# Opening, four feed-forward stages and two mixing stages in one block, the next stage's first products between the two turnings

## The reference, cut to what matters

```python
for l in range(2):                                   # first block
    x = layer_norm(ALPHA * x + 0.5 * ((silu(x @ ffn1_w1[l]) * (x @ ffn1_w3[l])) @ ffn1_w2[l]), ln1_g[l], ln1_b[l])
    h = x @ w_in[l]                                  # 1024 x 3360, split into the inputs of three mixers
    mix = concatenate([spatial_gating(..), gated_deltanet(..), gla(..)], -1) @ w_out[l]
    x = layer_norm(ALPHA * x + mix, ln2_g[l], ln2_b[l])
    x = layer_norm(ALPHA * x + 0.5 * ((silu(x @ ffn2_w1[l]) * (x @ ffn2_w3[l])) @ ffn2_w2[l]), ln3_g[l], ln3_b[l])
# second block: one layer
mod = silu(c) @ w_ada + b_ada                        # 1024 -> 6144: shifts, scales and gates
x = x + gate1 * attention(rms_norm(x) * (1 + scale1) + shift1)
y = x + gate2 * moe(rms_norm(x) * (1 + scale2) + shift2)   # 32 experts, 4 for each token, 1024 -> 2048 -> 1024
```

## Time and profile before

| | before |
|---|---|
| median of 3 runs | 2237.27 us (2235.18 to 2241.88) |
| the profiled execution's own time | 2240.23 us |
| its span, first to last instruction | 2238.5 us |
| mean granted TensorE clock | 0.996 |
| PE busy in the span | 2167.5 us (97%) |

### The profile page before, as it was taken

One profiled execution on the slowest core, in us unless ns is written; L12 is line 12 of the kernel. 1 busy time (PEld: TensorE's weight loads), 2 busy tenths in 40 slices (PEclk: granted clock), 3 DMA queues, 4 the chain that ended last, 5 costly groups with the idle time before them and its releaser, 6 DMA issues. The chain is left out here.

```text
span 2238.5 us, 30473 instructions
## 1 busy us (share of the span) xinstructions
PE 2167.5 (97%) x12481; PEld 1340.7 (60%) x12482; DVE 1025.8 (46%) x1421; ACT 726.6 (32%) x1121; POOL 92.1 (4%) x139
## 2 busy tenths in 40 slices
PE   8999999999999999999999999999999999999997
PEld 7887877888888887788877743333333333333332
DVE  5665686865666468766559642111111111111111
ACT  5443333643444243354335631111111111111111
POOL 5000020000000001100001000000000000000000
PEclk9999999999999999999999999999999999999999
DMA  9773422687386443158736669999999999999998
GB/s 308 237 237 98 151 78 72 227 284 243 104 298 223 151 145 114 40 185 273 240 129 186 244 277 423 428 429 428 428 429 428 429 428 428 429 428 428 429 429 336
DMA packets 192726, 632.40 MB, mean 283 GB/s; under 512 B 31280, under 2 KB 127552, under 8 KB 166256
## 3 DMA queue, kind: packets, MB, share of 16 engines
q1 hardware_dynamic: 192624, 630.93, 73.1%
HBM read 629.82 MB, written 1.07 MB: 282 GB/s over the span
## 5 line engine op out<-in xcount | busy, mean ns | idle before, releaser
L426 PE MATMUL banks<-ffn_room 128*128 128x512 f32 x1824 | 430.4, 391 | 0.0
L426 PEld LDWEIGHTS banks<-ffn_room 128*128 128x128 f32 x1824 | 339.5, 188 | 69.0
L546 DVE TENSOR_TENSOR ffn_room<-memory,ffn_room 128x2048 fp32r<-128x2048 f32 x132 | 298.7, 2291 | 92.9 <-ACT ffn_room L505 92.9
L3196 DVE TENSOR_SCALAR attend_words<-banks 128x512 f32<-128x512 f32 x32 | 22.1, 692 | 560.5 <-PE banks L2932 560.5
L505 ACT CAST ffn_room<-memory 128x2048 fp32r<-128x2048 f32 x132 | 247.1, 1905 | 68.5 <-PE banks L444 63.4
L444 PE MATMUL banks<-ffn_room 128*128 128x512 f32 x1056 | 248.1, 390 | 0.3
L2932 PE MATMUL banks<-memory 128*64 128x512 f32 x1088 | 242.7, 594 | 0.0
L444 PEld LDWEIGHTS banks<-ffn_room 128*128 128x128 f32 x1056 | 197.6, 188 | 42.7 <-DVE ffn_room L588 2.1
L2932 PEld LDWEIGHTS banks<-memory 128*64 128x64 f32 x1088 | 75.2, 135 | 150.6 <-issue 148.3
L2932 PE MATMUL banks<-attend_later,memory 128*64 128x512 f32 x672 | 152.1, 594 | 0.1
L511 ACT ACTIVATE memory<-banks 128x256 f32<-128x256 f32 x88 | 34.0, 386 | 324.6 <-PE banks L426 305.6
(11 more groups left out here) (478 smaller groups left out, 2780.1 us busy)
## 6 DMA issues: line engine op xcount, KB each, us to landing
memory<-in_ffn_w SPq DMA_DIRECT2D x132, 1024.0 KB, 7.5
memory<-in_w_gate_up SPq DMA_DIRECT2D x62, 2048.0 KB, 22.4
attend_later<-in_w_gate_up SPq DMA_DIRECT2D x39, 2048.0 KB, 23.9
memory<-in_w_down SPq DMA_DIRECT2D x25, 2048.0 KB, 24.2
attend_later<-in_w_down SPq DMA_DIRECT2D x19, 2048.0 KB, 23.0
attend_words<-in_w_gate_up SPq DMA_DIRECT2D x17, 2048.0 KB, 22.4
memory<-in_w_in SPq DMA_DIRECT2D x32, 1024.0 KB, 6.6
memory<-in_w_ada SPq DMA_DIRECT2D x32, 768.0 KB, 5.6
```

Source lines behind the costliest of these rows:

```text
L426: m = nc.tensor.matmul(psum[:, GU + tt, :], x_parts[:, xp, k, tt * P:tt * P + P], rows, start=(n == 0), stop=(n == 3 * KD - 1))
L546: tt_op(b, chip.ring[:, chip.slot(base + i), :], a.bitcast(F32), ALU.subtract).then_inc(chip.used, 1)
L3196: ts(room.gate, psum[:, GATE_BANK, :], 7.0, None, ALU.min).then_inc(s["g_ready"], 1)
```

## The change

All seven stages up to `attend_phase` are emitted into one block. The objects `Opening` and `PostNorm` hold the steps of a seam, and a stage's list calls those of the stage before (`before`) and of the stage after (`following`). Semaphores of the four feed-forward stages count on (`Sems.at`) and are not cleared between.

- PE, between the two turnings of a seam: `gate_up_plain` or `unit(0)` on row block 0. After a feed-forward stage (`pause` = 4) blocks 0 to 3 of the first tile come before the second turning and 4 to 7 after it. After a mixing stage (`pause` = 8) the whole first tile comes before. After the opening (`pause` = 0) none does. The filling products go, except 3 before `attend_phase`.
- After a mixing stage row block 0 is turned before `output(1, 3)`, and ACT scales all eight of its blocks.
- The first two tiles to be split of the next stage are cast and subtracted ahead: in the last step of a feed-forward stage, or in the tail of a mixing stage (there one subtraction only, `lows` = 1). `flip` chooses the free buffer.
- `xT` is split in halves of 128 tokens.
- In the opening c is asked for first, x as two loads, then the six tiles; a row block is turned when its load is there.
- SP's and GpSimd's lists of a stage wait for the second row block of `xT` (`ready_first`, `ready_last`); the last tile of the ring in a mixing stage waits for one count more.

```diff
+class PostNorm:
+
+
+    leads, lows = 2, 2
...
+    def blocks(self, act, tt, half):
+
+        chip, s, gbT = self.chip, self.s, self.chip.gbT
+        act.wait_ge(*s.at("norm_gbT", 32))
+        act.wait_ge(*s.at("x_turned", 2 * tt + half + 1))
+        for k in range(4 * half, 4 * half + 4):
+            m = self.nc.scalar.activation(chip.xT[:, k, tt * P:tt * P + P], chip.psum[:, 2 * tt + half, (k % 4) * P:(k % 4) * P + P],
+                                          ACT.Identity, bias=gbT[:, 1, k:k + 1], scale=gbT[:, 0, k:k + 1])
+        m.then_inc(s["xT_last" if half else "xT_first"], 1)
...
-    with nc.Block() as block:
+    norm = PostNorm(chip, s, chain, gamma_beta, [s.at("down", STEPS + i) for i in range(2 * NT)], skip, chip.eps[:, 1:2], 4)
+
+    def lead(act, i):
+
+        chip.arrived(act, base + i)
+        nc.scalar.copy(split_place(i)[0], chip.ring[:, chip.slot(base + i), :]).then_inc(s["lead"], 1)
+
+    def low(dve, i):
+
+        dve.wait_ge(*s.at("lead", split_done[i] + 1))
+        a, b = split_place(i)
+        nc.vector.tensor_tensor(b, chip.ring[:, chip.slot(base + i), :], a.bitcast(F32), ALU.subtract).then_inc(chip.used, 1)
+
+    def emit(block, before, following):
...
         @block.sync
         def _(sp):
             if rows_before:
+                before.ready_first(sp, 1)
+                before.ready_last(sp, 1)
...
+            before.ready_first(pe, 0)
+            if before.pause == KD:
+                before.ready_last(pe, 0)
+            if before.pause:
+                gate_up_plain(0, 0, before.pause)
+            before.turn(pe, 1)
+            before.ready_last(pe, 0)
+            if before.pause < KD:
+                gate_up_plain(0, before.pause, KD)
+            gate_up_plain(1, 0, KD)
             gate_then_up(0, 1)
...
-            n_tensor(pe)
+            norm.turn(pe, 0)
+            sum_ada(pe)
...
+            def x_lead(tt):
+                cols = slice(tt * P, tt * P + P)
+                before.ready_first(act, tt)
+                before.ready_last(act, tt)
+                nc.scalar.copy(x_parts[:, 0, :, cols], chip.xT[:, :, cols]).then_inc(s["x_lead"], 1)
...
-            nc.scalar.copy(x_parts[:, 0, :, :], chip.xT).then_inc(s["x_lead"], 1)
-            for i in range(4):
-                lead(i)
+            x_lead(0)
+            before.blocks(act, 1, 0)
+            x_lead(1)
+            for i in range(before.leads, 4):
+                lead(act, i)
             silu(0, 0)
-            lead(load_y(0))
+            lead(act, load_y(0))
             for ft in range(STEPS):
+                if ft + 1 == STEPS and following:
+                    following.early_lead(act, 0)
+                    following.early_lead(act, 1)
...
+            before.last_blocks(dve, 1)
+            x_low(0)
+            x_low(1)
+            for i in range(before.lows, 3):
+                low(dve, i)
...
+                if ft + 1 == STEPS and following:
+                    following.early_low(dve, 0)
                 product(ft, 1)
+                if ft + 1 == STEPS and following:
+                    following.early_low(dve, 1)
...
+class Opening:
+
+
+    leads, lows, pause = 0, 0, 0
...
-            sp.dma_start(chip.x, x_in.rearrange("b (t p) d -> p (b t) d", p=P)).then_inc(s["x"], 16)
-            chip.issue(sp, loads, 0, 2)
             sp.dma_start(c_rows, c_in.rearrange("b (k p) -> (b k) p", p=P)).then_inc(s["c"], 16)
-            chip.issue(sp, loads, 2, RING)
+            for tt in range(chip.NT):
+                sp.dma_start(chip.x[:, tt, :], x_in[0:1, tt * P:tt * P + P, :].rearrange("b p d -> p (b d)"))\
+                    .then_inc(s[f"x{tt}"], 16)
+            chip.issue(sp, loads, 0, RING)
...
-            pe.wait_ge(s["x"], 16)
             pe.wait_ge(s["ident"], 1)
...
+            nc.tensor.transpose(chip.psum[:, 4, 0:8], c_rows, chip.ident[0:8, 0:8]).then_inc(s["c_turned"], 1)
+            self.turn(pe, 0)
...
+            act.wait_ge(s["c_turned"], 1)
+            nc.scalar.activation(chip.cs, chip.psum[:, 4, 0:8], ACT.Silu).then_inc(s["c_made"], 1)
+            self.blocks(act, 0, 0)
...
+    norm = PostNorm(chip, s, chain, gamma_beta, [s.at("mixed", n) for n in (1, 1, 2)] + [(chip.used, end + 1)], skip, chip.eps[:, 0:1], KD)
+    norm.lows = 1
...
+            before.ready_first(sp_, 1)
+            before.ready_last(sp_, 1)
...
-            n_sync(sp_)
-            chip.issue(sp_, loads, base + RING, end + RING)
+            norm.ask(sp_)
+            chip.issue(sp_, loads, base + RING, end + RING - 1)
+            sp_.wait_ge(chip.used, end + 1)
+            chip.load(sp_, loads, end + RING - 1)
...
-            for n in range(4):
+            before.ready_first(pe, 0)
+            unit(0, 0, before.pause)
+            before.turn(pe, 1)
+            before.ready_last(pe, 0)
+            unit(0, before.pause, KD)
+            before.ready_first(pe, 1)
+            before.ready_last(pe, 1)
+            for n in range(1, 4):
                 unit(n)
...
+            norm.turn(pe, 0)
             output(1, 3)
-            n_tensor(pe)
...
-            copy(x_parts[0], chip.xT).then_inc(s["lead"], 1)
-            lead(1, 0)
-            lead(1, 1)
+            x_lead(0)
+            before.blocks(act, 1, 0)
+            x_lead(1)
             evac(0)
-            lead(2, 0)
-            lead(2, 1)
+            lead(act, 2, 0)
+            lead(act, 2, 1)
...
-            n_scalar(act)
+            following.early_lead(act, 0)
+            norm.deviation(act, 0)
+            norm.normalize(act, 0)
+            following.early_lead(act, 1)
+            norm.blocks(act, 0, 0)
+            norm.blocks(act, 0, 1)
+            norm.deviation(act, 1)
+            norm.normalize(act, 1)
...
-            n_vector(dve, chain, lambda: b_low(1))
+            norm.sums(dve, 0)
+            b_low(1)
+            norm.scaling(dve, 0)
+            dve.wait_ge(chip.used, end - 1)
+            following.early_low(dve, 0)
+            norm.sums(dve, 1)
+            norm.scaling(dve, 1)
+            norm.second_half()
...
+def close(chip, block, norm):
+
+
+    @block.tensor
+    def _(pe):
+        norm.turn(pe, 1)
+        fill(chip, 6, 3)
+
+    @block.scalar
+    def _(act):
+        norm.blocks(act, 1, 0)
+
+    @block.vector
+    def _(dve):
+        norm.last_blocks(dve, 1)
...
+        with nc.Block() as block:
+            before = Opening(chip, Sems(wide, START))
+            before.emit(block, a["x"], a["c_2"], loads)
+            for stage, following in zip(stages, stages[1:] + [None]):
+                stage.emit(block, before, following)
+                before = stage.norm
+            close(chip, block, before)
```

More of the change, by code:

```diff
@@ L329, in ffn_phase, with __init__ @@
+POST_NORM = "norm_gb norm_gbT variance deviation scaling normal x_new x_turned xT_first xT_last x_final"
+class Stage:
+    def __init__(self, norm, early_lead, early_low, emit):
+        self.norm, self.early_lead, self.early_low, self.emit = norm, early_lead, early_low, emit
+def ffn_phase(chip, s, chain, spent, l, loads, base, F, FT, gamma_beta, skip, room, flip, b_ada, rows_before, mod_before, on_gpsimd=None,
+              columns=()):
     nc, D, KD, NT = chip.nc, chip.D, chip.KD, chip.NT
@@ L3442, in ffn @@
             mod_before = mod_row[0:1, (n - 1) * ADA_BLOCK:n * ADA_BLOCK] if l and not i else None
-            with nc.sbuf_tensor(f"ffn_room_{l}_{i}", [P, chip.words - chip.fixed], F32R) as room:
-                ffn_phase(chip, sf, sm.span(), l, loads, base[3 * l + 2 * i], F, FFN_STEP, (a[norm + "_g"], a[norm + "_b"], l), 2 * alpha,
-                          room, a["b_ada_2"][0:1, block], rows_before, mod_before, on_gpsimd=on_gpsimd, columns=columns)
-            if i == 1 and l + 1 < DEPTH:
-                nc.all_engine_barrier(sems_to_clear=sf.span())
@@ L3458, in build @@
-        ffn(1, columns=[(chip.modT[:, i, :], v) for i, v in enumerate((a["norm1_g_2"][0:1, :], mod_row[0:1, D:2 * D],
-                                                                       mod_row[0:1, 0:D]))] if l + 1 == DEPTH else ())
+            weights = [a[f"ffn{i + 1}_{m}"] for m in ("w1", "w3", "w2")]
+            stages.append(ffn_phase(chip, s, ffn_chain, sm.span() if i or not l else None, l, loads, base[3 * l + 2 * i], F, FFN_STEP,
+                                    (a[norm + "_g"], a[norm + "_b"], l), 2 * alpha, low_room, i, a["b_ada_2"][0:1, part], rows_before,
+                                    mod_before, on_gpsimd=on_gpsimd, columns=columns))
```

481 lines of the change are left out of this document (252 added, 229 removed).

## The result

The changed kernel takes **2216.92 us** (median of 5 runs, 2214.48 to 2221.78) against 2237.27 before: ratio 0.9907, 95% interval 0.989 to 0.9925, so 20.8 us less, between 16.8 and 24.6. Forecast were 2218.7 us, range 2210 to 2232. The profiled execution took 2216.92 us with a span of 2215.1, 23.4 less than before's 2238.5.

The account below looks back on a forecast made before the run. PE was taken to bound the kernel until 1166 us and the experts' weight stream from 1345 us, its start set by PE. 5.1 + 2 x 1.9 + 2 x 3.6 + 2.5 = 18.6 us off 2237.3 gave 2218.7 us, range 2210 to 2232.

Parts of the forecast that it names:

- Rival 3: The gain is hidden by the experts' DMA stream, or lost in mixing through SP's later start: 2237 us, chance 0.11.
- The opening: Start of the kernel up to `gate_then_up`: 5.1 us gained, between 2.4 at worst and 6.2 at best.
- I take 16.5: Opening: chosen start of `gate_then_up` in us, nearer the best case because the new work has fewer holes.
- rival 1: Opening stays at 1.2 GHz as long after its first work as before, gaining 2.4 us: 2221.4 us, chance 0.15.
- Feed-forward into mixing: Two seams: half of `unit(0)` before the second turning, the rest after, PE without a stop: 1.9 us gained each.
- The SP delay: Seams into mixing: SP's small loads start 2.4 us later, delaying `finish_x`; DVE's 4.94 us wait covers it, priced at nothing.
- Mixing into feed-forward: Two seams: row block 0 turned before `output(1, 3)`, tile 0's products between the turnings: 3.6 us gained each.
- The next bound: Mixing into feed-forward: DVE's subtractions are the next limit, with a margin of 0.6 us.
- Rival 2: Seams join only in part, DVE's splits the next bound at the mixing seams: 2226 to 2229 us, chance 0.18.
- Between the layers: One seam, PE's order as at the other feed-forward seam, tile 0's instructions split in two: 2.5 us gained.
- Early splits: Before a feed-forward stage's last silu: no cost, since ACT waited 4.88 us and needs 3.8, DVE 4.58 and 2.3.
- rival 4: Early casts wait for next-stage tiles ahead of the last silu, holding PE's last turning: slower, 2249 us, chance 0.05.

Follow-up runs that it names:

- experiment 1: Changed kernel with the next stage's plain products behind both turnings at all five seams: three runs 2221.6 to 2224.5 us, five 2228.1 to 2231.7.
- experiment 3: Changed kernel without the early splits of the next stage's first tiles at the three seams into a feed-forward stage: 13.4 us slower in the medians.
- experiment 5: The changed kernel again, unaltered, on another chip and in more executions: 2215.69 us.
- experiment 11: Changed kernel plus three filling products in the opening and two among the router's logits: median 2214.48 us.
- experiment 4: Changed kernel with products behind both turnings, row block 0 turned after a mixing stage's last output product, and no early splits into feed-forward stages: 2231.32 us.
- experiment 10: Changed kernel with products behind both turnings, eight filling products before row block 1's turning at both mixing-into-feed-forward seams, three in the opening: median 2222.83 us.
- experiment 6: Changed kernel plus ten filling products in the opening, three before c's transposition and seven behind it: median 2215.67 us.
- experiment 9: Changed kernel plus three filling products in the opening, before c's transposition: median 2214.72 us.
- experiment 2: Changed kernel with row block 0's turning put back behind a mixing stage's last output product: median 2222.93 us.
- experiment 8: Changed kernel plus ten filling products in the opening and two among the router's logits: 2216.39 us.

## Why the prediction was right, and where it was off

**The bound** was read rightly: PE's work ahead of 1345 us sets when the stream starts, and the gain passed through one for one. Rival 3 is out.

**The opening (5.1)** was mis-sized for the first profile (3.3) and exact for another of the same program (5.15). The step that failed is "I take 16.5": forecast and rival 1 (the slow stretch stays) are not two answers but the two outcomes of one program. The price of rival 1 was also read wrongly. "Full pace came 10.7 us after the first work" joins two stretches: before's trace has an entry of 1.00 from 9.8 us on, while PE was waiting for c, and the clock fell to 0.50 at 13.2 us, as the next window shows, until 16.6.

```profile
12.00:14.00 2.00, 1.12 (x3) 0.91 (x4) 0.00 (x0) 1.10 (x2) 0.00 (x0) 0.79 1.09 346
```

So full pace came 3.8 us after the first work (5.92) and was lost again at the start of the plain products; in after's profile it came 8.5 us after it (13.3 less 4.88). That rival 1's 2.4 us lies near the 3.3 measured is luck. Of the seven profiles with this opening unaltered, `gate_then_up` came at 16.4 us in three (experiments 1, 3, 5) and at 18.3 to 18.9 in four; the plain products start at 9.6 us in the first and at 9.4 to 9.7 in the second, so the landing isn't what differs. The Trainium skill ("TensorE: Matmul & The Clock Gate", section "What's actually happening") says that activity releases the slow clock and that the number of slow products differs from run to run. The second agrees with these rows. The first does in the fact that every opening starts slow, but the release came after 3.8 us of work and waiting in before's profile and 12.7 us after the first filling in experiment 11's. A gain of 2.4 us, as I applied the rule, is near the 2.7 to 3.3 of four of these openings and far from the 5.2 of the other three.

**Feed-forward into mixing (1.9 each)** gave 2.2, by the steps named. The SP delay cost nothing, as said: `finish_x` came 2.6 us later relative to the seam, 2.4 forecast, and 0.90 of DVE's cover is left.

**Mixing into feed-forward (3.6 each)** gave 4.0. I put the start 9.1 us behind the last output product, it was 8.47. The next bound was not DVE's splits but x's second low part. Rival 2 did not occur, but experiment 3 shows that its mechanism is real: without the early splits PE waits 3.4 us for DVE's subtractions.

**Between the layers (2.5)** gave 2.65.

**Early splits** cost nothing in a last step (ACT still waits 2.02 us for PE in the first stage's, at 187.20 us), so rival 4 is out. But my sum didn't say what they are worth; undone they cost 8.0 us of waits and 4.1 of slow clock.

**The sum** came out closer than its terms: the opening gave 1.8 us less than forecast and the mixing stages 0.8, the seams 1.6 more. That part is luck.

**What I left out**: the clock. With neither fillings nor products in PE's wait at a mixing seam it fell (experiments 1 and 4), with eight fillings it stayed up (10), and so it did in the changed kernel, where real products took the fillings' place. And 4.3 of the profile's 23.4 us are before's own stretch of slow clock, not the change; so 19 is the better figure for it in these two profiles, near the runs' 20.8 (16.8 to 24.6) and the forecast's 18.6.

Open: the last 1.4 us in the experts; why the clock in the opening comes at 8 to 9 us in some executions and at 13.3 to 14.7 in others; whether five even runs at the logits are more than luck (without those fillings 5 of 19 runs of the changed kernel and of experiments 6 and 9 had a mean clock of 0.997 or less, with them none of 13).

## What to carry over

When a change takes filling out of PE's list, ask at each place whether products or a hole come in its stead: here a hole of 3.5 us cost 1.7 to 2.8 us more than itself in the profiled execution. Price a reordering and the early work that feeds it together: the new order without the early splits was 1.0 us faster than neither, both together 14.4. And where one term hangs on the clock at the start, say that both values will occur, and look at a second profile of the same kernel before explaining a difference of 2 us.

## What the runs showed of the hardware

- The granted clock falls with PE "busy": behind 32 products with 32 columns each it stood at 0.50 in several executions, for 10.2 us in before's. That the narrow products cause it is likely, not shown: two fillings among them left none in three profiles, but 3 of the 10 without fillings have none either.
- It also falls back within microseconds of having been given: 1.00, then 0.50 from about 9.6 us behind 1.61 us of idle PE, full again before 14 us (experiment 10). Behind a hole of 1.66 us in the same place it stayed (experiment 9), and of two holes of 2.66 us in one profile only the second was followed by a fall (experiment 2). Behind the six holes of 3.4 us or more at the mixing seams of experiments 1, 3 and 4 it fell each time.
- With PE at work nearly without a hole from 1.64 us on, full pace came between 6 and 7 us, both times (experiments 6 and 8). With three fillings from there on it came before 7 us in three profiles and not until 14.3 in one (experiment 11). With the turnings as its first real work (from 4.9 to 5.2 us) it was there at 9.6 us in three executions and only between 13.3 and 14.7 in four.
- DVE's operations with two SBUF operands took 1.76 us in place of 0.69 beside GpSimd's. Each mixing stage of every profile has two to four such slow ones of 128 x 512, at 1.64 to 1.77 us.
